# The norms ahead of block two: earlier weight splits, FFN down units by pairs, and the first token tile turned before the fourth unit

## The reference

```python
# end of first_block: FFN, then its norm and residual
f = (jax.nn.gelu(f_gate, approximate=True) * f_val) @ w_ffn_down[l]   # (256, 3072) @ (3072, 1024)
x = x + rmsnorm(f, ffn_post_norm[l])
# begin of second_block (_layer)
h = _rmsnorm(x, norm_pre)
cols = h @ w_in
mem_kv = _rmsnorm(mem, norm_mem) @ w_mem_kv
```

## Time and profile before

| what | value |
|---|---|
| median of 3 runs | 886.17 us (885.95 to 886.5) |
| profiled execution | 887.6 us, of which the span from first to last instruction is 885.8 us |
| PE busy | 859.1 us, 97% of the span |
| DVE busy | 635.3 us, 72% |
| ACT busy | 506.7 us, 57% |
| POOL busy | 71.7 us, 8% |
| granted TensorE clock, mean | 0.994 of full speed |

### The profile page before, as it was taken

One profiled execution on the slowest core, in us unless ns is written; L12 is line 12 of the kernel. 1 busy time (PEld: TensorE's weight loads), 2 busy tenths in 40 slices (PEclk: granted clock), 3 DMA queues, 4 the chain that ended last, 5 costly groups with the idle time before them and its releaser, 6 DMA issues.

```text
span 885.8 us, 14622 instructions
## 1 busy us (share of the span) xinstructions
PE 859.1 (97%) x5806; PEld 779.5 (88%) x5806; DVE 635.3 (72%) x1128; ACT 506.7 (57%) x821; POOL 71.7 (8%) x75
## 2 busy tenths in 40 slices
PE   6989999999999999999999899999999999999997
PEld 6979999999989999999998798899999776778885
DVE  6797987988867766656666898787456555775765
ACT  5565778665367755656657867535435434454443
POOL 0200001101020211111113000400000000000000
PEclk9999999999999999999999999999999999999999
DMA  9438543467455655565554547643432333355641
GB/s 343 154 121 301 169 143 120 154 203 265 156 175 184 221 191 177 184 205 171 191 188 145 181 152 242 208 147 103 123 107 94 98 112 97 124 196 196 197 149 48
DMA packets 40584, 149.19 MB, mean 168 GB/s; under 512 B 4520, under 2 KB 4676, under 8 KB 39876
## 3 DMA queue, kind: packets, MB, share of 16 engines
q1 hardware_dynamic: 40516, 148.25, 49.9%
HBM read 147.16 MB, written 1.08 MB: 167 GB/s over the span
## 4 chain that ended last, share of the span: by engine, by line
PE 84%; DVE 10%; ACT 4%; issue 1%; DMA 1%; SPq 0%; DVEq 0%; ACTq 0%
PE bank L607 39%; PE bank L602 15%; PE bank L604 14%; PE bank L603 14%; DVE t_wl L1709 3%; DVE t_arena L1724 3%; PE bank L610 2%; DVE t_arena L1714 1%; ACT t_hh L1216 1%; ACT t_wh L1211 1%; DVE t_x L1724 1%; DVE t_sm L1721 1%; ACT t_arena L1216 1%; DMA t_x<-in_xin 1%; ACT L1216 0%
## 5 line engine op out<-in xcount | busy, mean ns | idle before, releaser
L1709 DVE TENSOR_TENSOR t_wl<-t_raw,t_wh 128x1024 fp32r<-128x1024 f32 x260 | 316.6, 1227 | 111.9 <-ACT t_wh L1211 110.9
L1211 ACT ACTIVATE t_wh<-t_raw 128x1024 fp32r<-128x1024 f32 x260 | 272.9, 1058 | 124.4 <-PE bank L607 60.9
L602 PE MATMUL bank<-t_hh,t_wh 128*128 128x256 f32 x1144 | 331.3, 290 | 6.5 <-DVE t_wl L1709 2.8
L604 PE MATMUL bank<-t_hh,t_wl 128*128 128x256 f32 x1144 | 324.1, 283 | 0.0
L603 PE MATMUL bank<-t_hl,t_wh 128*128 128x256 f32 x1144 | 324.0, 283 | 0.0
L602 PEld LDWEIGHTS bank<-t_hh,t_wh 128*128 128x128 f32 x1144 | 219.7, 192 | 11.0 <-issue 6.1
L603 PEld LDWEIGHTS bank<-t_hl,t_wh 128*128 128x128 f32 x1144 | 219.9, 192 | 0.8
L604 PEld LDWEIGHTS bank<-t_hh,t_wl 128*128 128x128 f32 x1144 | 219.6, 192 | 0.0
L607 PE MATMUL bank<-t_wh,t_br 128*128 128x512 f32 x384 | 123.8, 393 | 0.2 <-POOL t_br L2426 0.2
L1724 DVE SCALAR_TENSOR_TENSOR t_arena<-bank,t_par,t_arena 128x255 f32<-128x255 f32 (+2 forms) x184 | 75.2, 473 | 40.9 <-ACT t_arena L1216 40.5
L607 PE MATMUL bank<-t_wh,t_hh 128*128 128x512 f32 x224 | 91.4, 408 | 1.7 <-DVE t_wl L1709 1.7
(11 more groups left out here) (142 smaller groups left out, 850.8 us busy)
## 6 DMA issues: line engine op xcount, KB each, us to landing
t_raw<-in_ws SPq DMA_DIRECT2D x260, 512.0 KB, 3.9
t_br<-decay SPq DMA_DIRECT2D x1, 2048.0 KB, 10.8
t_arena<-in_post SPq DMA_DIRECT2D x3, 512.0 KB, 4.6
t_arena<-gates SPq DMA_DIRECT2D x1, 1536.0 KB, 10.8
t_x<-in_xin SPq DMA_DIRECT2D x4, 256.0 KB, 5.8
t_bd<-in_bd SPq DMA_DIRECT2D x1, 1024.0 KB, 11.2
t_x<-in_xtok SPq DMA_DIRECT2D x1, 1024.0 KB, 5.9
t_arena<-in_mem SPq DMA_DIRECT2D x1, 1024.0 KB, 8.0
```

The costliest lines, as they stand in the source:

```text
L602: e.matmul(o, wh, xh, start=first, stop=False, skip_group_check=True)
L604: return e.matmul(o, wl, xh, start=False, stop=last, skip_group_check=True)
L1211: e.activation(WH[q % NS][:, :], RAW[q % NR][:, :], ACT.Copy, bias=0.0, scale=1.0).then_inc(*hi.now(q))
L1709: e.tensor_tensor(WL[q % NS][:, :], RAW[q % NR][:, :], WH[q % NS][:, :].bitcast(F), SUB).then_inc(*lo.now(q))
```

## The change

Three things change, all at the seam.

- On PE, the last four FFN down units (i = 0 to 3) are worked in another order of (tile, unit): the pair (1, 0) comes directly behind (0, 0), and (1, 1) behind (0, 1). PE's turn of tile 0 is issued ahead of its waits for m3's weights and for m3's moving data.
- The splits have other places in ACT's and DVE's norm: m0 and m1 both ahead of it; m2 between x_squares(0, 0) and the squares of tile 1's second half; m3 behind tile 0's second root on ACT, and behind DVE's scaled of tile 0. DVE's row_bias for tile 1's second norm moves behind m3's split.
- The split of n2 (q + 6) is no longer part of the norm, on either engine: it follows behind the high and low parts of h, at the next `walk.unit()` that reaches it.

```diff
@@ pe_program
-            for tt, i in ((0, 0), (0, 1), (1, 0), (0, 2), (0, 3), (1, 1), (1, 2), (1, 3)):
+            for tt, i in ((0, 0), (1, 0), (0, 1), (1, 1), (0, 2), (0, 3), (1, 2), (1, 3)):
...
                     u = walk.unit()
+                    if i == 1 and j == 1:
+                        turn_rows("pre2", 0)()
                     split_ready(u)
                     e.wait_ge(*g_mh.of(2, 2 * i + j))
-                    if i == 1 and j == 1:
-                        turn_rows("pre2", 0)()
@@ act_program, token_norm
-                kept, last, ready = {"fpre": (4, "mk1", q + 5), "pre2": (6, "mk3", q + 6)}[pre]
+                kept, last, ready = {"fpre": (4, "mk1", q + 5), "pre2": (6, "mk3", q + 5)}[pre]
                 if pre == "pre2":
-                    walk.ahead(q)
+                    walk.ahead(q + 1)
                 post_squares(post, 0, 0)
                 post_squares(post, 0, 1)
                 root(post, 0, 0)
                 walk.ahead(q + 1)
                 post_squares(post, 1, 0)
                 x_squares(post, pre, 0, 0)
+                if pre == "pre2":
+                    walk.ahead(q + 2)
                 post_squares(post, 1, 1)
                 root(post, 0, 1)
                 x_squares(post, pre, 0, 1)
                 root(pre, 1, 0)
-                walk.ahead(q + 2)
+                walk.ahead(q + (3 if pre == "pre2" else 2))
                 x_squares(post, pre, 1, 0)
@@ dve_program, token_norm
                 if pre == "pre2":
-                    walk.ahead(q)
+                    walk.ahead(q + 1)
...
                 row_bias(pre, 1, 0)
+                if pre == "pre2":
+                    walk.ahead(q + 2)
                 weighted(post, 1, 1)
                 row_rsqrt(post, 0, 1)
                 post_added(post, 1)
-                walk.ahead(q + 2)
-                row_bias(pre, 1, 1)
-                row_rsqrt(pre, 1, 0)
-                scaled(pre, 0)
+                if pre == "pre2":
+                    row_rsqrt(pre, 1, 0)
+                    scaled(pre, 0)
+                    walk.ahead(q + 3)
+                    row_bias(pre, 1, 1)
+                else:
+                    walk.ahead(q + 2)
+                    row_bias(pre, 1, 1)
+                    row_rsqrt(pre, 1, 0)
+                    scaled(pre, 0)
                 row_rsqrt(pre, 1, 1)
                 scaled(pre, 1)
-                walk.ahead(q + 5 if pre == "fpre" else q + 6)
+                walk.ahead(q + 5)
```

## The result

The changed kernel takes 890.62 us in the median (890.5 to 891.08, 4 runs) against 886.34 for the kernel before: a ratio of 1.0045, 95% interval 1.0033 to 1.0057. Slower was forecast, by 2.4 us (888.6, range 885.5 to 889.6); the time lies a microsecond above the range. Run a second time it gave 1.0043 (1.0031 to 1.0055).

A forecast was written before the change was run, and what follows sets the result against it. The prediction took the norm's chain to set h's start, with PE busy 97% of the span. Terms of +0.1 (h's start), +1.3 (clock) and +1.0 us (n2's split) raised 886.17 to 888.6 us, range 885.5 to 889.6.

The forecast's parts named there:

- What bounds, PE's order of pairs: On PE at the seam: at most 2.6 us of waits to remove; the new order starts m0 0.4 us sooner.
- The splits and the norm, on DVE: DVE's queue at the seam: two splits beside POOL take 1.26 us each; its half of tile 0 ends at 493.30.
- +0.1 for h's start: At the end of PE's second turn, which releases the high parts of h: they start 0.1 us later.
- What is late next: ACT's half of tile 0: its root waits for row_bias behind m3's split, so PE's turn starts at about 495.6.
- One wait in place of two: PE ahead of the turn: one 3.4 us wait replaces 1.65 and 0.77; clock falls to 1.2 GHz, costing 1.3 us.
- n2's split: Behind the seam: moved behind h, it delays the chain on ACT and DVE; PE's wait grows by 1.0 us.
- The sum: Whole execution: 0.1, 1.3 and 1.0 us make +2.4 us, from 886.17 to 888.6 us.
- dearer case: Rival, behind the seam: the clock falls again or bank 1 isn't free for n1, another 1.3: 889.9 us; chance 10%.
- The reference time: Whole execution: medians lie 1.4 us under the profiled execution of 887.6 us; this difference was carried over to the forecast.

The follow-up runs named there:

- the filler kernel: Changed kernel with 14 matmuls of 512 columns added on PE between m2 and the turn of tile 0; 888.41 us, ratio 1.0019.
- the kernel with row_bias early: Changed kernel with DVE's row_bias of tile 1 put ahead of scaled(pre, 0) and of m3's split; 887.02 us, ratio 1.0005.

## Why the prediction was wrong

- **What bounds, PE's order of pairs: right.** The norm's chain set h's start. m0 starts 483.72 - 477.54 = 6.18 us behind A (6.61 before): 0.43 for 0.4. In the changed kernel nothing of it arrives, since ACT's scaled half releases the turn 3.20 us behind m2; no run has the pairs' order alone. The other half of PE's part, the turn ahead of m3's weights, gains nothing here as forecast, but on the kernel before the two together gave 0.82 us at H.
- **The splits and the norm, on DVE: the step that failed.** The step read: "A split with POOL at work beside it takes 482.25 - 480.93 less the row_bias between (0.06), 1.26 us. Two now: 480.93 + 2.52 = 483.45." The row is read rightly, but it is that of the engine that began first: POOL's subtraction beside it took 2.30 us instead of 1.3, and I didn't look at POOL's rows. The second split, which began behind POOL's, took 2.31 us. The term "+0.1 for h's start" is measured at 22.18 - 21.15 = +1.03 us (from the filler kernel, in which the chain is as late and the clock doesn't fall). Moving the split away from POOL gave 1.10 us at H, and holding POOL back took the pair from 3.58 to 2.48 us. The remaining steps behind it were right to 0.1 us: take the 0.99 away and the turn would stand 17.8 behind A, where 495.6 - 477.77 was forecast.
- **What is late next: right.** The root waited for row_bias behind m3's split, 1.75 us; taking that away alone gave 2.5 us.
- **One wait in place of two: right in kind.** 3.20 us, forecast 3.4; PE also waited 0.79 us at m2, which I had at none, because of the same late split. The clock fell, and cost 1.43 us; forecast 1.3. That the size came out so near is partly luck. In the row it was taken from (49.53) the clock's 1.3 us cost the kernel nothing: from that matmul to A it takes 428.20 to 428.25 us in all 13 profiles, whether the clock fell there or not, because PE waits again behind it. At the seam the slow work lay on the path to h. Nor did the price scatter from profile to profile: in the six profiles in which the clock fell, the turn to H takes 4.83 to 5.00 us, against 3.40.
- **n2's split: right.** 0.87 us, forecast 1.0, in full and once.
- **The sum.** 0.1 + 1.3 + 1.0 was 2.4; measured 1.03 + 1.43 + 0.87 = 3.33. The difference of 0.93 us is the split beside POOL; that the clock cost 0.13 more and n2's split 0.13 less cancels. The range was too narrow above for the same reason: its dearer case was another fall of the clock or a busy bank, and no bound was set on the price of the second split, though the kernel before had never put two there.
- **The reference time.** The profiled execution of before was 1.4 us above its median, and I carried that over. It was a run in which the clock fell twice early on (from 15 to 18 and from 49 to 52 us), and of the two only the first can have made it longer (last section). The medians of the two kernels lie 3.9 to 4.3 us apart, the seam explains 3.3 to 3.5, and the rest is within the interval.

The Trainium skill has the rule that I had not weighed (SBUF — State Buffer, "SBUF: two separate sides"): a DVE instruction with two inputs in SBUF and a GpSimd instruction that reads SBUF take one shared pair of ports in turn, each for its whole length, and whichever starts first holds up the other. The runs here agree: splits and post_added were held up, weighted with an operand in PSUM was not, and POOL's halves in place of wholes shortened the second split by 0.55 us.

## What to carry to other kernels

Ahead of moving an instruction, ask of each engine beside the new place whether it competes with it, and price it from rows in which the same two lie together, and read them for both: the one that begins first shows no price while the other pays it (1.33 us and 2.30 us here). Where two engines hand small values to each other, look at what stands in front of the small instruction: 0.15 us of row_bias behind a 1.2 us split held ACT, then PE, and then the clock. Two short waits can be cheaper than one long: 1.65 and 0.77 us kept the clock here, 3.20 lost it. A split moved out of an idle stretch into a busy queue was paid in full at the next place where PE waits for that queue (0.87 us).

## What the runs showed of the hardware

The same wait gives different clocks. In all 13 profiles (those of the kernels before and after, and of the 11 runs above) PE waits 2.39 to 2.42 us ahead of the same matmul, which starts at 47.5 to 49.6 us. In eight of them the stretch from 50 to 51 us was at 0.50 (as in the kernel before, and here in the changed kernel), in five at full speed (here the kernel with row_bias early, whose row shows 1.00):

```profile
49.31 0.55 PE L602 MATMUL bank<-t_hh,t_wh 128*128 128x256 f32 x1 [2.42 <-DVE t_arena L1716]
```

```profile
47.52 0.35 PE L602 MATMUL bank<-t_hh,t_wh 128*128 128x256 f32 x1 [2.40 <-DVE t_arena L1716]
...
50.00:51.00 1.00, 0.63 (x6) 0.42 (x4) 1.00 (x4) 0.41 (x1) 0.00 (x0) 1.00 0.00 0
```

In the five that kept the clock the wait ended by 47.91 us, in the eight others at 48.67 or later: the wait is equally long but lies elsewhere in the span. That fits the free-running monitor that the prediction cited from the Trainium skill (TensorE: Matmul & The Clock Gate, "Part 1: The HAM clock gate"), though no run sets the place on purpose. At the seam the clock fell in all five profiles with a wait of 3.16 to 3.20 us and in the one with 2.33, and in none of those with waits up to 1.65.

This fall isn't what scatters the start of A between 475.8 and 477.8 us. The scatter is there by the time of PE's 61st matmul, which starts at 16.9 to 19.0 us; from it to A the 13 profiles agree to 0.05 us (458.84 to 458.89). Part of it is an earlier fall: in the five profiles with A at 477.4 us or later the clock was at 0.50 from 15 to 17 us too, in the eight others at 1.00. What sets the others apart (three at 476.9 to 477.0, five at 475.8 to 476.2) stays open. So single profiles of this kernel differ by 2 us for a reason that no edit made; distances between two events past the first 20 us compare well.
